# Expert 0's token rows gathered already transposed: eight pairs of strided-stationary matmuls, placed around the expert's first weight blocks

## The reference, cut to what matters

```
h = rmsnorm(x, ffn_norm_g)                       # x: 256 x 1024, float32
logits = h @ w_router + b_router                 # 32 experts
top 4 of them, weights = softmax(top values)
for each expert e, for the rows of its tokens:
    u = h_rows @ w_up[e] + b_up[e]               # 1024 x 2048
    a = clamped_swiglu(u)                        # pairs of columns: gate, up
    y = a @ w_down[e] + b_down[e]                # 1024 x 1024
    x[token] += weight * y
out = rmsnorm(x, final_norm_g)
```

## Time and profile before

| | us |
|---|---|
| median of 3 runs | 1063.95 |
| lowest and highest of them | 1063.81 and 1064.26 |
| the profiled execution's own time | 1064.09 |
| its span, first to last instruction | 1062.0 |
| PE busy (share of the span) | 1033.2 (97%) |
| PE weight loads busy | 408.6 (38%) |
| DVE busy | 203.9 (19%) |
| ACT busy | 155.8 (15%) |
| read from HBM | 421.70 MB |

### The profile page before, as it was taken

The page is one execution under the profiler, slowest core; times in us unless marked ns, Lnnn a source line. Parts: engine busy times, 40 slices in busy tenths (PEclk is TensorE's granted clock), DMA queues, the critical chain, the costliest instruction groups (busy, mean ns, idle before and its releaser), DMA issues.

```text
span 1062.0 us, 12731 instructions
## 1 busy us (share of the span) xinstructions
PE 1033.2 (97%) x5102; PEld 408.6 (38%) x5102; DVE 203.9 (19%) x603; ACT 155.8 (15%) x394; POOL 20.9 (2%) x49
## 2 busy tenths in 40 slices
PE   9999999999999999999999999999999999999996
PEld 7777653333333333333333233333333333333332
DVE  3434532111111111111111011111121101011112
ACT  2334441111111111111111001111100101011102
POOL 5001000000000000000000000000000000000000
PEclk9999999999999999999999999999999999999999
DMA  9993489999999999999999999999999999999995
GB/s 285 321 357 106 187 329 369 422 429 427 433 430 433 430 431 429 434 431 430 433 430 432 432 432 433 432 431 431 431 432 431 431 434 428 429 430 431 425 424 219
DMA packets 37544, 423.35 MB, mean 399 GB/s; under 512 B 8560, under 2 KB 12704, under 8 KB 19840
## 3 DMA queue, kind: packets, MB, share of 16 engines
q1 hardware_dynamic: 36992, 422.34, 94.9%
q10 hardware_dynamic: 512, 0.42, 0.2%
HBM read 421.70 MB, written 1.05 MB: 398 GB/s over the span
## 4 chain that ended last, share of the span: by engine, by line
PE 76%; DMA 21%; DVE 1%; ACT 0%; issue 0%; DVEq 0%; SPq 0%; POOL 0%; POOLq 0%
PE ps L1289 28%; DMA ring<-in_w_up_dram 21%; PE ps L1322 17%; PE ps L1336 5%; PE ps L1217 4%; PE ps L1015 4%; PE ps L1112 3%; PE ps L1022 2%; PE ps L1242 2%; PE ps L1271 1%; PE ps L1258 1%; PE ps L1308 1%; DVE work L1818 1%; PE ps L1139 1%; PE ps L1302 1%; PE ps L1128 1%
## 5 line engine op out<-in xcount | busy, mean ns | idle before, releaser
L1289 PE MATMUL ps<-ring,work 128*64 128x512 f32 x1888 | 421.0, 602 | 13.8 <-DMA ring<-in_w_up_dram 13.8
L1289 PEld LDWEIGHTS ps<-ring,work 128*64 128x64 f32 x1888 | 133.4, 138 | 299.2 <-issue 273.4
L1322 PE MATMUL ps<-ring,work 128*64 128x512 f32 x1008 | 223.3, 595 | 3.1 <-DVE work L1818 1.0
L1789 DVE TENSOR_SCALAR work<-ps 128x512 f32<-128x512 f32 x31 | 21.4, 691 | 611.3 <-PE ps L1289 604.4
L1322 PEld LDWEIGHTS ps<-ring,work 128*64 128x64 f32 x1008 | 70.0, 137 | 136.7 <-issue 127.7
L881 ACT ACTIVATE work<-work 128x512 f32<-128x512 f32 x31 | 19.5, 630 | 449.2 <-DVE work L1789 449.2
L1336 PE MATMUL ps<-work 64*128 64x512 f32 x256 | 63.6, 615 | 0.7 <-ACT work L897 0.7
L1217 PE MATMUL ps<-xt,work 128*64 128x512 f32 x256 | 60.7, 593 | 1.0 <-ACT work L897 0.8
L897 ACT ACTIVATE work<-ps 128x512 f32<-128x512 f32 x32 | 19.1, 597 | 229.9 <-PE ps L1322 229.9
L1015 PE MATMUL ps<-extra,ring 128*128 128x256 f32 x192 | 43.0, 380 | 0.0
L1336 PEld LDWEIGHTS ps<-work 64*128 64x128 f32 x256 | 22.0, 186 | 41.8 <-issue 40.2
(11 more groups left out here) (267 smaller groups left out, 548.4 us busy)
## 6 DMA issues: line engine op xcount, KB each, us to landing
ring<-in_w_up_dram SPq DMA_DIRECT2D x48, 4096.0 KB, 37.2
ring<-in_w_down_dram SPq DMA_DIRECT2D x24, 4096.0 KB, 36.4
ring<-in_w_up_dram SPq DMA_DIRECT2D x20, 2048.0 KB, 16.3
ring<-in_w_up_dram SPq DMA_DIRECT2D x19, 1024.0 KB, 9.9
ring<-in_w_down_dram SPq DMA_DIRECT2D x9, 2048.0 KB, 16.2
ring<-in_w_down_dram SPq DMA_DIRECT2D x12, 1024.0 KB, 9.1
ring<-in_w_in_dram SPq DMA_DIRECT2D x6, 1024.0 KB, 11.2
ring<-in_w_out_dram SPq DMA_DIRECT2D x4, 512.0 KB, 10.0
```

The source lines that it names most:

```text
L1289: t = pe.matmul(UP[h * 64:h * 64 + 64, a, :], xgT[:, k, :], row[:, a * 64:(a + 1) * 64, h, :], start=False, stop=(k == KD - 1), skip_group ...
L1322: t = pe.matmul(ps[h * 64:(h + 1) * 64, XG, :], aT[:, j, u * 64:u * 64 + 64], w[:, j * D + h * 512:j * D + (h + 1) * 512], start=(u == 0 a ...
L1789: dve.tensor_scalar(t1, up_pairs[:, 0], 7.0, None, ALU.min).then_inc(swi, 1)
```

## The change

For block 0 alone, `gather_tile`, ACT's copies and the four transposes are replaced by `gather_first`: now `xt` is the stationary operand, 128 columns with a step of 4 elements (16 bytes), and `pm[:, n, :]` (64 columns) the moving one, so that the result is transposed from the start. Each piece j takes four matmuls: two halves h for each of the two tiles n; 16 matmuls in all, that is 32 records. The pieces lie in banks 0, 1, 6, 7 (`FIRST`). Tile 0's eight matmuls stand around the `PLACES[1]` matmul, where tile 0's gather and `keep_warm` stood; tile 1's stand behind `pm_ready`, those of pieces 0 and 2 ahead of row block 0, and those of pieces 3 and 1 behind it. Row block 0 now starts the accumulation (`start=(k == 0)`); the bias comes behind row block 2 and adds. Row block 6 moves ahead of block 1's gather. `xg_done` and `xg_read` count one less. ACT's two copies are gone.

```diff
-        FIRST = [4, 5, 6, 7]
+        FIRST = [0, 1, 6, 7]
...
-            act.wait_ge(xg_done, 1)
-            for i in range(2):
-                act.activation(xg.rearrange("q (j p) -> q j p", j=4)[:, i::2],
-                               ps[:, XG, :].rearrange("q (p j) -> q j p", j=4)[:, i::2], ACT.Copy)\
-                   .then_inc((first_copied, xg_read)[i], 1)
...
+            def gather_first(n, js):
+
+                for j in js:
+                    for h in range(2):
+                        t = pe.matmul(ps[:, FIRST[j], h * 64:(h + 1) * 64],
+                                      xt[:, n, h * 512 + j:(h + 1) * 512:4], pm[:, n, :],
+                                      start=(n == 0 and h == 0), stop=(n == 1),
+                                      skip_group_check=True)
+                    if n == 1:
+                        t.then_inc(first_turned if j != 1 else xgT_done, 1)
...
-            def up_bias(b, prev, UP=UP):
+            def up_bias(b, prev, UP=UP, start=True):
...
-                                      start=True, stop=False, skip_group_check=True)
+                                      start=start, stop=False, skip_group_check=True)
...
-                                          start=False, stop=(k == 7), skip_group_check=True)
+                                          start=(k == 0), stop=(k == 7), skip_group_check=True)
...
-            gather_tile(0)
+            gather_first(0, (0, 2, 3))
             pe.wait_ge(m_ready, 2)
             pe.matmul(ps[:, PLACES[1], 0:E], upper[:], M[:, 1, :], start=False, stop=True).then_inc(pos_done, 1)
-            keep_warm(2)
+            gather_first(0, (1,))
             pe.wait_ge(pm_ready, 1)
-            gather_tile(1).then_inc(xg_done, 1)
-            up_bias(0, False)
-            pe.wait_ge(first_copied, 1)
-            for i, j in enumerate((0, 2, 3, 1)):
-                if i == 2:
-                    pe.wait_ge(xg_read, 1)
-                pe.transpose(ps[:, FIRST[j], 0:P], xg[:, j * P:(j + 1) * P], ident[:, :])\
-                  .then_inc(first_turned if i < 3 else xgT_done, 1)
-            up_first(in_singles(0), (0, 2, 3, 4, 5))
+            gather_first(1, (0, 2))
+            up_first(in_singles(0), (0,))
+            gather_first(1, (3, 1))
+            up_first(in_singles(0), (2,))
+            up_bias(0, False, start=False)
+            up_first(in_singles(0), (3, 4, 5, 6))
             gather(1, first=True)
-            up_first(in_singles(0), (1, 6))
+            up_first(in_singles(0), (1,))
             gather_turn(1)
             up_first(in_singles(0), (7,))
             up_bias(1, False, UP1)
```

More of the change, by code:

```diff
@@ L332, in hybrid_layer @@
         first_down_used = sem("first_down_used")
-        first_copied = sem("first_copied")
         first_turned = sem("first_turned")
@@ L872, in read_xg @@
             def read_xg(b):
-                act.wait_ge(xg_done, b + 1)
+                act.wait_ge(xg_done, b)
                 act.activation(xg.rearrange("q (j p) -> q j p", j=4),
@@ L1209, in fold @@
                   .then_inc(logits_done, 1)
-            def keep_warm(n):
-                for _ in range(n):
-                    pe.matmul(ps[:, OUT[0][0], 0:P], ident[:, :], ones[:], start=True, stop=True)
+            def gather_first(n, js):
[7 more added lines that the diff above has]
+                        t.then_inc(first_turned if j != 1 else xgT_done, 1)
             def gather_tile(n):
@@ L1229, in gather_turn @@
             def gather_turn(b):
-                pe.wait_ge(xg_read, b + 1)
+                pe.wait_ge(xg_read, b)
                 for j in range(4):
@@ L1299, in combine_turn @@
                 pe.wait_ge(pw_ready, b + 1)
-                pe.wait_ge(xg_read, b + 1 + ahead)
+                pe.wait_ge(xg_read, b + ahead)
                 for n in range(NT):
@@ L1835, in _ @@
                .then_inc(w_ready, 1)
-            dve.wait_ge(xg_done, 1)
             pick(1, listed(1))
@@ L1841, in _ @@
             read_xgT(1, xgT1)
-            dve.wait_ge(xg_done, 2)
+            dve.wait_ge(xg_done, 1)
             pick(2, listed(2))
@@ L1854, in listing @@
                 weigh(i, i, listed(i))
-                dve.wait_ge(xg_done, i + 1)
+                dve.wait_ge(xg_done, i)
                 pick(i + 1, listed(i + 1))
@@ L1913, in _ @@
                     e = dve.value_load(ovi[0:1, ds(o, 1)], min_val=0, max_val=E - 1)
-                    dve.wait_ge(xg_done, o + E)
+                    dve.wait_ge(xg_done, o + (E - 1))
                     dve.wait_ge(cT_done, o + E)
```

## The result

The changed kernel takes 1070.06 us (median of 5, 1069.52 to 1070.86), the kernel before in the same comparison 1064.26 (1063.81 to 1067.89): **1.0049 times as long, 95% interval 1.0036 to 1.0061**. Forecast were 1062.3 us and a range up to 1064.9. It is slower by 5.8 us; what came nearest was rival C, the slow strided load, and that was too small as well.

A forecast was written before the change was run, and what follows sets the result against it. The transfer stream was taken to bound the kernel; row block 0 starting 1.72 us earlier would close its last hole, passing 1.7 us through whole: 1063.95 to 1062.25, stated as 1062.3 us, range 1061.7 to 1064.9.

The forecast's parts named there:

- rival C: New gather's strided weight loads take twice as long, 0.22 us a record; 1064.6 to 1064.9 us; chance 0.18.
- What bounds the kernel: Expert part from about 182 us: the full transfer stream sets the end; PE has 13.8 us to spare.
- The step of a weight load: New gather's 32 records: 0.11 us each, taken from rows of contiguous 128 x 128 loads.
- What is put between: PE behind row block 0: eight records 0.88 us, bias 1.02, reordered row blocks; PE as a whole 0.19 us later.
- No piece can land sooner than about 4.6 us after its issue: Block 0's weight pieces: landing bound from piece 1 with the queue empty; slack 2.7 us at piece 6, 2.3 at 8.
- the 1.7 us at piece 1: Piece 1 lands at about 165.0 rather than 166.7 us, and this gain passes through whole to the end.
- rival B: Stream follows issues of pieces 6 to 8, of which 7 and 8 come 0.19 us later; 1063.9 to 1064.2 us; chance 0.15.
- If the stream then loses as much at the lower rate as it did: Stream behind piece 1: the same loss from the 359 GB/s stretch as before, so piece 8 lands at 184.7 us.
- a constant rate: Stream from about 182 us on: a constant number of bytes at 430 GB/s, then a constant PE tail.
- its way of being wrong altogether: Forecast's stated failure condition: the stream has another hole behind 182 us.
- Rival D: The 359 GB/s stretch comes from the hole and goes with it; gain 2.1 us, 1061.8 us; chance 0.10.
- the tail behind 980.5 us: PE work at the end, waiting for no transfer, taken to be of constant length.

The follow-up runs named there:

- e3: Changed kernel with neighbouring columns as stationary operand and each of the 16 gather matmuls done twice (expert 0's rows wrong); 1069.52 us in one run.
- e8: Changed kernel, step of four kept, with the bias split in halves, the first ahead of row block 0; 1073.74 us in one run.
- e1: Changed kernel with 128 neighbouring columns instead of every fourth as stationary operand (expert 0's rows wrong); 1066.05 us, ratio 1.0009 to the kernel before.
- e2: Changed kernel with every second column as stationary operand (step of 8 bytes, expert 0's rows wrong); 1068.70 us in one run.
- e10: Changed kernel, step of four kept, with two dense 512-column matmuls added, results unused, ahead of and within the gather; 1072.31 us in one run.
- e9: e4 with two dense 512-column matmuls added, at PE's waits for ACT and for tile 1's place matrix; 1066.60 us, ratio 1.0026 to the kernel before.
- e16: The changed kernel unchanged, run again for a second profile; 1072.09 us.
- e4: Changed kernel with neighbouring columns made right by loading expert 0's w_up rows and gains in that order; 1066.66 us, ratio 1.0017 to the kernel before.
- e11: e4 with one dense 512-column matmul added at PE's wait for ACT ahead of the last router step; 1067.46 us in one run.
- e12: e11 with block 1's gather moved from behind row block 6 to behind row block 3; 1067.28 us, ratio 1.0028 to the kernel before.
- e6: Kernel before without its two keep_warm matmuls; 1064.03 us in one run, the kernel before 1064.00.
- e14: Kernel before with SP issuing piece 6 only when row block 7 has been read, 2.45 us later; 1065.83 us, ratio 1.0009.
- e5: e4 with the bias split in halves, the first ahead of row block 0; 1070.77 us, ratio 1.0053 to the kernel before.
- e7: Kernel before with only row block 6 moved ahead of block 1's gather; 1064.80 us in one run, the kernel before 1064.00.

## Why the prediction was wrong, point by point

**What bounds the kernel: right.** The end follows the stream of transfers. The bytes missing at 200 us, at 430 GB/s, give the delay of the last wait within 1.3 us in 16 of the 17 other profiles (e3: 2.1), from 11.79 MB and 990.2 us (e8) to 15.52 MB and 980.5. PE's own work isn't what ends last, with 13.6 us to spare in the changed kernel too; its lateness acts through the places that it frees.

**"The step of a weight load ... I take 0.11": the first step that failed.** It is 0.23. The rows that I took it from have no step between columns, and I said so; I took the value that they bound from below, without evidence for this pattern, although the Trainium skill's rule (as cited in the prediction) names exactly this case, and gave it 0.18. e1 and e2 show it. Rival C had the mechanism and the place right: it had L1440 1.22 us late (1.36 in the trace: 2.78 behind the start of the gather for 1.42), and piece 8 issued 2.8 us behind the forecast's time, where e10 against e9 has 3.5. Of the end the step has 1.9 to 2.5 us by the traces of e10 and e9, and some 4 by the repeated runs of the changed kernel and e1: the largest part either way, its size not settled.

**TensorE's clock: in no term at all.** I never looked at what PE streams in the stretch, only at how long it takes. Taking 512 moving columns out of a stretch that is already lean brought the clock to 1.2 GHz for 6.9 us (e16: 13.6 us), and row block 0 took 3.05 us to the next row for 1.87. By piece 1's issue that costs PE 1.2 us, 1.5 in e4 (7.25 against e11's 5.76), and piece 8 is issued 2.0 later still where the low clock reaches row block 2 (e16's 32.04 against 30.07). What of it reaches the end is not settled. Counted from the records ahead of the added matmuls (L1187 to L1195), the last wait ends at 829.38 in e4 and 829.19 in e11, at 831.77 in the changed kernel and 832.60 in e10, but at 835.66 in e16, where the clock was low for longest. The added matmuls themselves cost 0.66 us, and a second one 0.4 more; by the repeated runs e9 and e12, with the clock up, are no faster than e4. I called `keep_warm` no more than something to be replaced, which e6 bears out; what the new order took away was the gather's 512 moving columns.

**"What is put between": undersized.** Eight records and row block 2 take 2.90 us rather than 2.60, bias and row block 3 2.89 rather than 2.74 (e11, clock held, no step). From row block 0 to the gather, and from row block 2 to the bias, it is 1.87 us from start to start, not the 1.72 from row block to row block, and the gather's eight records take 1.04, not 0.88: 0.15 at each such passage. The kernel before had shown it, in row block 7 and the bias behind it:

```profile
174.62 1.94 PE L1258 MATMUL ps<-ring,work 128*64 128x512 f32 x8
176.49 1.09 PE L1242 MATMUL ps<-work 32*64 32x512 f32 x8
```

With 0.15 more ahead of piece 1, PE was 0.78 us late at piece 8 in e11, not 0.19.

**"No piece can land sooner than about 4.6 us after its issue": the wrong rule for slack.** I took the slack as landing less (issue + 4.6), 2.7 and 2.3 us. But the stream runs dry about 2 us ahead of the last landing: some 1.3 us of slack at piece 6 (e14). If piece 8's was too large by the same 1.4, it was 0.9 and not 2.3 (an estimate), and the 1.7 us at piece 1 could not have passed through whole, even with the clock and the loads as I had them. What came is rival B's sign: in e11 piece 8 lands 31.8 us behind the gather's start, before 31.6, though piece 1 had been issued 1.6 us sooner from there. Its mechanism is not borne out: it gave each piece 6.9 to 7.3 us of its own, and e14's piece 6 took 4.8.

**"If the stream then loses as much at the lower rate as it did" and "a constant rate" from 182 us on: not so.** From 163 to 182 us the kernel before moved 394 GB/s and e11 370, and every profile with the new gather stays at 342 to 396 from 180 to 190 us. So the stream had a loss behind 182 us too, which the forecast had named as its way of being wrong altogether. With the step and the clock's fall both gone, the last wait ends 2.0 to 3.1 us later than before, counted as above (829.05, 829.19 and 830.15 in e12, e11 and e9 for 827.03), and not 1.7 sooner; the added matmuls can account for 0.7 to 1.1 of it. Rival D, less of the low rate, has it the wrong way round.

**The clock behind the last wait** took 1.7 us of the first profile's 6.0. The forecast held the tail behind 980.5 us to be constant; it is 81.5 us or 83.2.

What stays open: why the stream runs at some 370 GB/s with a full share until about 190 us in every kernel with the new gather, where the kernel before is at 426 from 176 us on. Several causes are out. It isn't piece 1 being issued early (it is late in the changed kernel, e5 and e8), nor pieces 2 and 3 being 2.9 us apart (1.7 in e5 and e8), nor the long pause ahead of piece 7 (e7 has the pause and 418 GB/s, e12 has a shorter one and 385). What the twelve share is that PE is 0.8 us or more late at piece 7, the bias behind row block 2 or split, and the new gather itself; none of these was tried alone.

## What to carry to other kernels

Where no row shows a new operand pattern and a rule speaks against it, put the expensive side into the sum, not the cheap one: a stationary operand with one float32 in each 16 bytes took twice as long to load here, two in 16 bytes were nearly free. Where an edit takes wide matmuls out of a stretch of small ones, look at what TensorE streams there, not only at how long it is busy; one dense matmul ahead of the stretch held the clock where those behind it didn't. But count what it costs from a point ahead of it: here it took 0.66 us of the 1.2 to 1.5 that it was to give back, and nothing was left that the runs could show. And measure a stream's slack by when its rate drops, in bytes, not by landings.

## What the runs showed of the hardware that I had not expected

- A load of 128 float32 columns, 128 rows: 0.11 us a record with neighbouring columns, 0.12 with a step of two, 0.23 with a step of four. At the lower clock the first takes 0.21 (e5) and the last is unchanged, 0.23 (the changed kernel, e8): it isn't TensorE's clock that limits it.
- TensorE's clock can fall although PE is marked busy for 100% of the time (154.2 to 162.9 us), and stay up although it is idle for 0.7 us (e6).
- Behind a wait of 2 us for a transfer the clock fell in five of ten profiles, on the same row of the program: 8.78 us for it (idle 2.04, changed kernel) or 7.09 (idle 2.40, kernel before).
- A stream with a DMA share of 0.99 to 1.00 can be at 370 GB/s (e11) or at 430 (kernel before); the share alone doesn't say which.
